# A hybrid encoder layer: the first 512 tokens turned and multiplied unscaled in the first pair of column tiles

## Chip, cores and metric

One Trainium2 chip, one core. The metric is the device time of one execution in microseconds (us), the median of several runs.

## What is computed

One encoder layer on x (1024 tokens x 1024 channels, float32), cut to what the change touches:

```
h    = x * rsqrt(mean(x*x over the channels) + 1e-6) * g_pre     # one inverse root for each token
proj = h @ w_in                                                  # 1024 x 7424 columns
q, k, v, gates, z, ... = split(proj)
q, k = partial_rope(q), partial_rope(k)                          # 16 of each head's 64 rows turn with the position
```

Behind it stand three branches (a short gated convolution; attention over a window of 128 tokens to each side, with a sink; cross-attention into 256 memory tokens), their up-projections, the merge by sigmoid gates, the output projection and `x + rms_norm(out)`. The inverse root of a token is a factor of its whole row of `h`, and so of its column in each tile of `proj`, which the kernel keeps transposed (channels on the partitions, tokens along the row).

## The kernel before

**Precision.** Each float32 operand is split into a high and a low float32r part. A product is three passes on TensorE: high x high, high x low, low x high. ScalarE makes the high parts (`high_part`, L1204, of weights; `high_of_h`, L1225, of h), and the low ones, operand minus high, are GpSimd's (`low_part`, L764; `low_of_h`, L769) or VectorE's.

**The start.** SyncE loads x in eight blocks of 128 tokens (L501 to L508), the weights of the first pair between them. ScalarE squares each block (`square_sum`, L1214; VectorE block 4), VectorE and ScalarE make the inverse roots (`variances`, `roots`, `inverses`), and the blocks are scaled in place: 0, 1, 2 and 4 by VectorE, 3, 6 and 7 by ScalarE, 5 by GpSimd. `turn_x` (L943) transposes chunk n: chunk 0 to 7 is 128 channels of tokens 0 to 511, 8 to 15 the same channels of tokens 512 to 1023. It takes four transposes into one of four PSUM banks (`spare`, by n % 4). From the bank ScalarE makes the high part with g_pre as its scale; VectorE makes the low part and, for n < 8, the float32 copy (`copy_h`, L1574); for n >= 8 the copy is ScalarE's (L1231). For the chunks of `POOL_CHUNKS` the low part is made by GpSimd from the copy. TensorE works off warm-up products (`warm`, L1082) in three batches until data are there.

**Column tiles.** The projection's 58 tiles of 128 columns go in pairs. The first three pairs (`P_DIRECT`) are multiplied directly: pair 0 by `first_pair` (L882), chunk by chunk, each chunk used for both tiles (six passes of 512 tokens), with the transposes of a later chunk ahead of it; pairs 1 and 2 by `direct_pair` (L907), a tile at a time, each of 48 + 48 passes over its two halves of weights. The rest are Strassen products (seven in place of eight), for which VectorE combines the four quarters of h: `sum_t1`, `sum_t3`, `sum_t2`, `sum_t4` (L1589 to L1612), each in four steps of 128x512.

**Order on VectorE.** Its list (L1725 to L1773) is worked off in this order: the lows and copies of the 16 chunks with the root work between them; T1 and T3, then T2, 12 sums; then for tile 0 (k) `swap_rows(0)`, `times_cos(0)`, `rotate(0)`: a shuffle of rows from PSUM, a product with the cosine table, one with the sine table and their sum, each 128x1024. The lows of combinations and the other four rotary tiles follow. A tile's PSUM bank is free when its cosine product is made: TensorE's tile 3 waits for `cos_made` 1, tile 4 for 2, tile 5 for 3 (L910 to L912). Only tiles T_K, T_Q to T_Q + 3 turn with the position; the first pair holds T_K and T_Q, and tile 2 is T_Q + 1.

**From the rotary tiles to attention.** ScalarE (`rope_high`, L1279) and GpSimd (`rope_low`, L785) split each tile, in their lists between parts of weights; SyncE stores the parts in DRAM (`store_rope`, L485) and, when the first four are stored, loads the first block for attention (`load_block(0)`, L541: q_d, kh_d, kl_d). TensorE's first scores (L977) wait for these three.

**Waits between engines** are on counted semaphores; each engine works its list strictly in order.

## Time and profile before

| | us |
|---|---|
| median of 3 runs (lowest, highest) | 926.87 (926.81, 927.2) |
| the profiled execution's own time | 925.96 |
| its span, first to last instruction | 924.1 |
| busy: TensorE / VectorE / ScalarE / GpSimd | 907.8 / 657.1 / 439.2 / 453.4 |
| mean granted TensorE clock | 0.996 |

The busy times are sums over the span. TensorE's is 98% of it, but the end of a matmul is modelled, so a busy engine need not be at its peak. A row of a timeline gives start, length, engine, line, operation, output and input; one that joins several instructions has their number behind an x. In a row the time in square brackets is idle time of the engine ahead of it.

### The profile page before, as it was taken

The page shows a single profiled execution, that of the slowest core. Times are in us where ns is not written, and L with a number is a line of the kernel's source. Part 1 is how long each engine was busy: PE and PEld are TensorE (multiplying, and loading weights), DVE is VectorE, ACT ScalarE, POOL GpSimd, SP SyncE. Part 2 cuts the span into 40 slices and gives each one's busy share as a digit, 9 for nine tenths or more (in the row PEclk, how much of TensorE's full clock was granted, in tenths as well). Part 3 has the DMA queues.
Part 4 walks back from the last instruction along what each step waited for, and adds up shares of the span by engine and source line. Part 5 has one row for each costly group of instructions (what it writes and reads, how often), then busy time and mean ns, then how long its engine had stood idle before and what let it go on. Part 6 is the DMA issues. An engine that isn't in the chain of part 4 may idle for free.

```text
span 924.1 us, 12763 instructions
## 1 busy us (share of the span) xinstructions
PE 907.8 (98%) x4376; PEld 763.3 (83%) x4376; DVE 657.1 (71%) x1060; ACT 439.2 (48%) x849; POOL 453.4 (49%) x303
## 2 busy tenths in 40 slices
PE   9999999999999999999999999999999999999995
PEld 8788788888888888888888888888888888888784
DVE  5689976565656566656576178888797358899887
ACT  7624464444444466544463434343444544445341
POOL 3546844444444444444446744444443636668452
PEclk9999999999999999999999999999999999999998
DMA  7243846252525242525255322222222974750333
GB/s 287 96 116 83 228 144 210 90 171 91 170 91 169 96 128 102 193 91 171 108 174 174 116 80 80 79 78 82 80 69 68 333 262 143 258 181 0 142 110 137
DMA packets 82336, 126.56 MB, mean 137 GB/s; under 512 B 7136, under 2 KB 40544, under 8 KB 82272
## 3 DMA queue, kind: packets, MB, share of 16 engines
q1 hardware_dynamic: 81952, 125.61, 41.2%
q8 instruction: 36, 0.59, 0.2%
q14 instruction: 28, 0.23, 0.1%
q10 hardware_dynamic: 320, 0.13, 0.1%
HBM read 92.56 MB, written 33.55 MB: 136 GB/s over the span
## 4 chain that ended last, share of the span: by engine, by line
PE 81%; DVE 8%; ACT 3%; DMA 3%; POOL 2%; issue 2%; SPq 1%; DVEq 0%; ACTq 0%
PE pm L866 17%; PE pm L864 17%; PE pm L865 17%; PE pm L1162 3%; PE pm L1163 3%; PE pm L1161 3%; PE pv L999 2%; PE sa L987 2%; PE sa L1163 2%; PE sa L1162 2%; PE sa L1161 2%; PE pv L1078 2%; PE sa L1058 1%; DVE area L2158 1%; DVE area L2135 1%
## 5 line engine op out<-in xcount | busy, mean ns | idle before, releaser
L766 POOL TENSOR_TENSOR ring<-spots,ring 128x512 fp32r<-128x512 f32 x234 | 340.9, 1460 | 389.9 <-ACT ring L1207 377.9
L864 PE MATMUL pm<-hc,ring 128*128 128x512 f32 x784 | 308.6, 394 | 0.0
L866 PE MATMUL pm<-hc,ring 128*128 128x512 f32 x784 | 305.8, 390 | 0.0
L865 PE MATMUL pm<-hc,ring 128*128 128x512 f32 x784 | 305.5, 390 | 0.0
L1207 ACT ACTIVATE ring<-spots 128x512 fp32r<-128x512 f32 x234 | 146.2, 628 | 268.6 <-PE pm L866 177.5
L866 PEld LDWEIGHTS pm<-hc,ring 128*128 128x128 f32 x784 | 147.2, 188 | 31.2
L864 PEld LDWEIGHTS pm<-hc,ring 128*128 128x128 f32 x784 | 147.3, 188 | 29.3 <-issue 0.6
L865 PEld LDWEIGHTS pm<-hc,ring 128*128 128x128 f32 x784 | 147.4, 188 | 28.9
L1161 PE MATMUL pm<-hc,ring 128*128 128x512 f32 x128 | 49.9, 390 | 0.0
L1162 PE MATMUL pm<-hc,ring 128*128 128x512 f32 x128 | 49.8, 389 | 0.0
L1163 PE MATMUL pm<-hc,ring 128*128 128x512 f32 x128 | 49.8, 389 | 0.0
L766 POOL TENSOR_TENSOR ring<-area,ring 128x512 fp32r<-128x512 f32 x28 | 41.6, 1484 | 12.2 <-ACT ring L1207 11.1
L1826 DVE TENSOR_TENSOR area<-pv,area 64x512 f32<-64x512 f32 x16 | 11.0, 689 | 49.1 <-ACT area L1334 49.1
L1664 DVE TENSOR_TENSOR snaps<-pm,snaps 128x512 f32<-128x512 f32 x26 | 17.9, 690 | 37.9 <-PE pm L866 37.8
L1457 ACT ACTIVATE area<-area 128x1024 f32<-128x1024 f32 x24 | 25.4, 1057 | 38.0 <-DMA area<-raw_d 38.0
L1212 ACT COPY snaps<-pm 128x512 f32<-128x512 f32 x26 | 15.3, 588 | 45.9 <-PE pm L866 45.9
L1341 ACT ACTIVATE area<-area,st 128x384 f32<-128x384 f32 (+1 forms) x64 | 36.7, 574 | 0.0
L1676 DVE TENSOR_TENSOR area<-pm,snaps 128x512 f32<-128x512 f32 x26 | 17.9, 690 | 24.4 <-PE pm L866 24.2
L1658 DVE TENSOR_TENSOR snaps<-pm,snaps 128x512 f32<-128x512 f32 x26 | 18.0, 691 | 23.3 <-PE pm L866 23.3
L1653 DVE TENSOR_TENSOR area<-pm,snaps 128x512 f32<-128x512 f32 x26 | 18.0, 692 | 21.7 <-PE pm L866 17.3
L1349 ACT ACTIVATE area<-area,st 128x384 f32<-128x384 f32 (+1 forms) x64 | 32.5, 579 | 0.8 <-DVE st L1812 0.6
L1628 DVE TENSOR_TENSOR spots<-spots 128x512 f32<-128x512 f32 x26 | 30.6, 1176 | 0.9
(248 smaller groups left out, 1664.5 us busy)
## 6 DMA issues: line engine op xcount, KB each, us to landing
spots<-in_w SPq DMA_DIRECT2D x116, 256.0 KB, 3.2
raw_d<-area SPq DMA_DIRECT2D x72, 256.0 KB, 2.0
area<-raw_d SPq DMA_DIRECT2D x24, 512.0 KB, 4.4
area<-in_x SPq DMA_DIRECT2D x16, 512.0 KB, 4.2
spots<-in_wup SPq DMA_DIRECT2D x24, 256.0 KB, 4.5
spots<-in_wout SPq DMA_DIRECT2D x20, 256.0 KB, 3.7
q_d<-area_r SPq DMA_DIRECT2D x16, 256.0 KB, 4.3
area<-raw_d SPq DMA_DIRECT2D x16, 256.0 KB, 3.6
```

The source lines that it names most:

```text
L766: nc.gpsimd.tensor_tensor(ring_part(n, 1), operand(n), ring_part(n, 0).bitcast(F32), ALU.subtract).then_inc(lo_made, 1)
L864: pe.matmul(bank, hi, moving_hi(k), start=(k == 0), stop=False)
L865: pe.matmul(bank, hi, moving_lo(k), start=False, stop=False)
L866: mm = pe.matmul(bank, lo, moving_hi(k), start=False, stop=(k == HC - 1))
L1161: pe.matmul(dst, hi, y[:, at, 0, cols], start=(begin and c == chunks[0]), stop=False)
L1162: pe.matmul(dst, hi, y[:, at, 1, cols], start=False, stop=False)
L1163: mm = pe.matmul(dst, lo, y[:, at, 0, cols], start=False, stop=(end and c == chunks[-1]))
L1207: nc.scalar.activation(ring_part(n, 0), operand(n), ACT.Copy).then_inc(hi_made, 1)
L1341: ins = nc.scalar.activation(row, row, ACT.Exp, bias=st[:, 3, h:h + 1], accum_out=st[:, 5, h:h + 1])
L1349: ins = nc.scalar.activation(row, row, ACT.Copy, scale=st[:, 6, h:h + 1])
L1457: nc.scalar.activation(gate_of(g), gate_of(g), ACT.Sigmoid).then_inc(gate_sig, 1)
L1628: nc.vector.tensor_tensor(spots[:, A21, :], spots[:, A11, :], spots[:, A21, :], ALU.subtract).then_inc(s_made, 1)
```

## The change

Tokens 0 to 511 are no longer scaled before they are turned. SyncE brings them in four pieces of 256 channels (`load_columns`), so that chunks 0 and 1 can be turned when the first piece is there; blocks 4 to 7 come by rows as before and are scaled before they are turned (4, 5 and 6 by VectorE, 7 by ScalarE). The first pair of tiles is multiplied with the unscaled chunks 0 to 7 in its first half. ScalarE now makes all 16 high parts and all 16 copies; of the squares, VectorE has blocks 4, 5, 7, 0 and 1 and ScalarE 6, 2 and 3. The inverse roots of tokens 0 to 511 are laid out as rows (`inverse_rows`) and spread over all partitions by four transposes into a PSUM bank (`spread_inverses`), ahead of chunk 13. With them VectorE scales the copies of chunks 0 to 7 (`normalise`), and their high and low parts are made once more (`high_of_normal`, `low_of_normal`, the latter on VectorE for chunks 0, 2, 4, 6 and on GpSimd for 1, 3, 5, 7); tile 2 runs its scaled second half of tokens first (`second_side`). The output of the first pair gets its factors in the rotary step: the first halves of the cosine and sine tables are multiplied by the inverse roots (`scale_tables`), and `times_cos` and `rotate` of the first two tiles go in two halves. The warm-up is one batch of 32 steps in place of 28, 8 and 4. Chunks from 8 on use three PSUM banks. Several semaphores are joined (memory and output variances and roots), with waits in the same places.

The diff, cut to its core:

```diff
-WARM_STEPS = (28, 8, 4)
-ROOT_GROUPS = (slice(0, 2), slice(2, 4), slice(4, NB))
-POOL_CHUNKS = (2, 6, 8, 10, 12, 14)
+WARM_STEPS = 32
+ROOT_GROUPS = (slice(4, 6), slice(6, NB), slice(0, 4))
+MEM_ROOT = len(ROOT_GROUPS) + 1
+POOL_CHUNKS = (4, 6, 10, 12, 14)
+POOL_NORMALS = (1, 3, 5, 7)
+TURNS_AT = {0: (), 1: (2, 3), 2: (4,), 3: (5,), 4: (6,), 5: (7,), 8: (9, 10), 9: (11,), 10: (12,), 11: (13,),
+            12: (14,), 13: (15,)}
+SPREAD_BEFORE = 13
+SQUARES = (4, 5, 7, 0, 1)
...
+def spare_of(n):
+    return n % 4 if n < KC else (n + 2) % 3
+def bank_before(n):
+    return n - 4 if n < KC else {KC: 5, KC + 1: 6, KC + 2: 4}.get(n, n - 3)
+def turn_no(n):
+    return n + 1 + (n >= SPREAD_BEFORE)
...
+        raw_cos, raw_sin = spots[:, S1, :], spots[:, S2, :]
...
+            def load_columns(pair):
+                cols = slice(2 * pair * P, 2 * (pair + 1) * P)
+                sp.dma_start(f32(X0, 4 * D).rearrange("p (b d) -> p b d", b=4)[:, :, cols],
+                             x[0:4 * P, cols].rearrange("(b p) d -> p b d", p=P)).then_inc(x_landed[pair], 16)
+            def load_x(b):
                 sp.dma_start(f32(X0 + b * D, D), x[b * P:(b + 1) * P, :]).then_inc(x_landed[b], 16)
+            load_spot(A11, 0)
+            load_columns(0)
             sp.dma_start(ident[:, :], ident_in).then_inc(ident_landed, 16)
             sp.dma_start(gpre[:, :], g_pre).then_inc(ident_landed, 16)
-            load_spot(A11, 0)
             load_spot(A21, 0)
-            for b in range(4, NB):
-                sp.dma_start(f32(X0 + b * D, D), x[b * P:(b + 1) * P, :]).then_inc(x_landed[b], 16)
+            load_columns(1)
             load_spot(A12, 0)
+            load_columns(2)
+            load_x(4)
             load_spot(A22, 0)
+            load_x(5)
+            load_columns(3)
+            load_x(6)
+            load_x(7)
...
+            sp.wait_ge(x_turned, 2 * KC + 1)
...
             nc.gpsimd.memset(snaps[:, 0, 0:P], 0.0).then_inc(warm_made, 1)
-            pool.wait_ge(xs_made, 2)
             low_part(0)
             low_part(1)
-            low_of_h(2)
             low_part(2)
             low_part(3)
-            pool.wait_ge(inv_made, 2)
-            nc.gpsimd.tensor_scalar(f32(X0 + 5 * D, D), f32(X0 + 5 * D, D), st[:, 9, 5:6], None,
-                                    ALU.mult).then_inc(xs_pool, 1)
-            for n in POOL_CHUNKS[1:]:
+            for n in POOL_CHUNKS:
                 low_of_h(n)
             low_part(4)
             low_part(5)
+            for n in POOL_NORMALS:
+                low_of_normal(n)
...
+                    for m in TURNS_AT.get(n, ()):
+                        if m == SPREAD_BEFORE:
+                            spread_inverses()
+                        turn_x(m)
...
+                        if n == KC - 1 and side == 1:
+                            turn_x(KC)
...
+            def second_side():
+                names = [(DIRECT[c], half) for half in (1, 0) for c in range(2)]
+                for name, half in names:
+                    n, c = AT[(1, name)], DIRECT.index(name)
+                    if half:
+                        pe.wait_ge(hi_made, n + 1)
+                        pe.wait_ge(lo_made, n + 1)
+                    elif c == 0:
+                        pe.wait_ge(n_hi, KC)
+                        pe.wait_ge(n_lo_pool, len(POOL_NORMALS))
+                        pe.wait_ge(n_lo_dve, KC - len(POOL_NORMALS))
+                    for k in range(HC):
+                        mm = direct(1, name, half, k, tile_bank(2), c == 0 and k == 0, c == 1 and k == HC - 1)
+                    if half == 0:
+                        mm.then_inc(slot_done, 1)
...
+            def spread_inverses():
+                pe.wait_ge(xs_made, 3)
+                pe.wait_ge(h_copied, KC)
+                pe.wait_ge(h_lo_dve, h_lo_count(KC - 1, h_lo_dve))
+                for b in range(4):
+                    mm = pe.transpose(pv[:, b * P:(b + 1) * P], snaps[:, 2, b * P:(b + 1) * P], ident[:, :])
+                mm.then_inc(x_turned, 1)
...
+            warm(WARM_STEPS)
             pe.wait_ge(ident_landed, 32)
-            for pair in range(2):
-                pe.wait_ge(xs_made, pair + 1)
-                if pair:
-                    pe.wait_ge(xs_act, 1)
-                for n in range(4):
-                    turn_x(n, (pair,))
-                warm(WARM_STEPS[pair + 1])
+            turn_x(0)
+            turn_x(1)
...
+                if n not in POOL_CHUNKS:
+                    act.wait_ge(h_lo_dve, h_lo_count(n, h_lo_dve))
+                nc.scalar.activation(f32(H_BLOCKS[n][2], HALF), spare[spare_of(n)], ACT.Identity,
+                                     scale=gpre[:, n % KC:n % KC + 1]).then_inc(h_copied, 1)
+            def high_of_normal(n):
+                idx, j, place = H_BLOCKS[n]
+                act.wait_ge(n_made, n + 1)
+                act.wait_ge(raw_used, 1)
+                nc.scalar.activation(hc[:, idx, 0, j, :], f32(place, HALF), ACT.Copy).then_inc(n_hi, 1)
...
-            for b in range(4):
-                square_sum(b)
-                if b % 2:
-                    roots(b // 2)
             high_part(0)
-            high_part(1)
-            act.wait_ge(inv_made, 1)
-            nc.scalar.activation(f32(X0 + 3 * D, D), f32(X0 + 3 * D, D), ACT.Copy,
-                                 scale=st[:, 9, 3:4]).then_inc(xs_act, 1)
             act.wait_ge(ident_landed, 32)
             for n in range(2 * KC):
                 high_of_h(n)
-                if n >= KC:
+                if n < 3:
+                    high_part(n + 1)
+                if n and n - 1 not in POOL_CHUNKS:
+                    copy_h(n - 1)
+                if n in POOL_CHUNKS:
                     copy_h(n)
-                if n == 1:
-                    square_sum(5)
-                if n == 2:
+                if n == 5:
+                    roots(0)
                     square_sum(6)
-                    high_part(2)
-                if n == 3:
-                    square_sum(7)
-                    high_part(3)
+                elif n == 6:
+                    roots(1)
+                elif n == 7:
+                    act.wait_ge(inv_made, 2)
+                    nc.scalar.activation(f32(X0 + 7 * D, D), f32(X0 + 7 * D, D), ACT.Copy,
+                                         scale=st[:, 9, 7:8]).then_inc(xs_act, 1)
+                elif n == 8:
+                    square_sum(2)
+                elif n == 9:
+                    square_sum(3)
+                elif n == 10:
                     roots(2)
-                if n == 5:
-                    act.wait_ge(inv_made, 2)
-                    for b in range(6, NB):
-                        ins = nc.scalar.activation(f32(X0 + b * D, D), f32(X0 + b * D, D), ACT.Copy,
-                                                   scale=st[:, 9, b:b + 1])
-                    ins.then_inc(xs_act, 1)
-                if n == 2 * KC - 2:
-                    high_part(4)
-                    high_part(5)
+                elif n in (13, 14):
+                    high_part(n - 9)
+            copy_h(2 * KC - 1)
+            for n in range(KC):
+                high_of_normal(n)
...
+            def low_of_h(n):
+                idx, j, _ = H_BLOCKS[n]
+                dve.wait_ge(h_hi_made, n + 1)
+                nc.vector.scalar_tensor_tensor(out=hc[:, idx, 1, j, :], in0=spare[spare_of(n)],
+                                               scalar=gpre[:, n % KC:n % KC + 1],
+                                               in1=hc[:, idx, 0, j, :].bitcast(F32), op0=ALU.mult,
+                                               op1=ALU.subtract).then_inc(h_lo_dve, 1)
+            def inverse_rows():
+                for b in range(4):
+                    ins = nc.vector.tensor_scalar(snaps[:, 2, b * P:(b + 1) * P], ident[:, :], 0.0, st[:, 9, b:b + 1],
+                                                  ALU.mult, ALU.add)
+                ins.then_inc(xs_made, 1)
+            def normalise(n):
+                place = f32(H_BLOCKS[n][2], HALF)
+                dve.wait_ge(x_turned, SPREAD_BEFORE + 1)
+                dve.wait_ge(h_copied, n + 1)
+                dve.wait_ge(h_lo_pool, h_lo_count(KC - 1, h_lo_pool))
+                nc.vector.tensor_tensor(place, place, pv[:, :], ALU.mult).then_inc(n_made, 1)
+            def low_of_normal(n):
                 idx, j, place = H_BLOCKS[n]
-                g = gpre[:, n % KC:n % KC + 1]
-                if n < KC:
-                    dve.wait_ge(h_hi_made, n + 1)
-                elif n % 2:
-                    dve.wait_ge(h_copied_act, n - KC + 1)
-                if n not in POOL_CHUNKS:
-                    nc.vector.scalar_tensor_tensor(out=hc[:, idx, 1, j, :], in0=spare[n % 4], scalar=g,
-                                                   in1=hc[:, idx, 0, j, :].bitcast(F32), op0=ALU.mult,
-                                                   op1=ALU.subtract).then_inc(h_lo_dve, 1)
-                if n < KC:
-                    nc.vector.tensor_scalar(f32(place, HALF), spare[n % 4], g, None, ALU.mult).then_inc(h_copied, 1)
+                dve.wait_ge(n_hi, n + 1)
+                nc.vector.tensor_tensor(hc[:, idx, 1, j, :], f32(place, HALF), hc[:, idx, 0, j, :].bitcast(F32),
+                                        ALU.subtract).then_inc(n_lo_dve, 1)
+            def scale_tables():
+                dve.wait_ge(rope_landed, 32)
+                for place, table in ((raw_cos, cosb), (raw_sin, sinb)):
+                    ins = nc.vector.tensor_tensor(place, table[:, 0:HALF], pv[:, :], ALU.mult)
+                link(ins)
...
                 b11, b12 = f32(B11F + j * HALF, HALF), f32(B12F + j * HALF, HALF)
-                dve.wait_ge(h_copied, j + 1)
-                dve.wait_ge(h_copied_act, j + 1)
-                dve.wait_ge(h_lo_pool, h_lo_count(HC, h_lo_pool))
+                dve.wait_ge(h_copied, KC + j + 1)
+                dve.wait_ge(n_made, j + 1)
+                dve.wait_ge(n_lo_pool, 2)
+                dve.wait_ge(n_lo_dve, 2)
...
+                if j < 2:
+                    nc.vector.tensor_tensor(rotated(j)[:, 0:HALF], tile_bank(t)[:, 0:HALF], raw_cos, ALU.mult)
+                    ins = nc.vector.tensor_tensor(rotated(j)[:, HALF:SEQ], tile_bank(t)[:, HALF:SEQ],
+                                                  cosb[:, HALF:SEQ], ALU.mult)
+                else:
+                    ins = nc.vector.tensor_tensor(rotated(j), tile_bank(t), cosb, ALU.mult)
...
+            low_of_h(0)
+            low_of_h(1)
+            low_of_h(2)
+            square_sum(4)
+            low_of_h(3)
+            square_sum(5)
             variances(0)
+            low_of_h(5)
             inverses(0)
-            scale_x((0, 1))
+            square_sum(7)
             variances(1)
+            scale_x((4, 5))
             inverses(1)
-            scale_x((2,))
-            square_sum(4)
-            for n in range(2 * KC):
-                copy_h(n)
-                if n == 3:
-                    variances(2)
-                    inverses(2)
-                if n == 4:
-                    scale_x((4,))
-                if n > KC + HC:
-                    sum_t1(n - KC - HC - 1)
-                    sum_t3(n - KC - HC - 1)
-            sum_t1(HC - 1)
-            sum_t3(HC - 1)
+            scale_x((6,))
+            low_of_h(7)
+            low_of_h(8)
+            square_sum(0)
+            low_of_h(9)
+            square_sum(1)
+            variances(2)
+            inverses(2)
+            inverse_rows()
+            low_of_h(11)
+            normalise(0)
+            normalise(1)
+            low_of_h(13)
+            for n in range(2, 5):
+                normalise(n)
+            low_of_h(15)
+            for n in range(5, KC):
+                normalise(n)
+            low_of_normal(0)
+            low_of_normal(2)
+            scale_tables()
+            low_of_normal(4)
+            low_of_normal(6)
+            for j in range(HC):
+                sum_t1(j)
+                sum_t3(j)
```

## Rows read from the trace of the kernel before

**Rows 1.** Waits of TensorE over the whole run: us in total, times, longest.

```profile
PE sa L864 <- DVE snaps L2186: 1.8, 1, 1.8
PE sa L977 <- DMA area_r<-kl_d: 1.5, 1, 1.5
...
PE pm L876 <- issue: 0.6, 1, 0.6
```

**Rows 2.** Stages: each engine's busy time, granted clock, DMA share, GB/s.

```profile
37.00:50.00 13.00, 13.00 (x61) 10.75 (x61) 13.00 (x14) 6.84 (x12) 8.44 (x5) 1.00 0.45 163
50.00:115.00 65.00, 63.47 (x285) 52.12 (x283) 60.37 (x69) 26.26 (x41) 43.56 (x23) 1.00 0.54 141
115.00:863.00 748.00, 747.84 (x3613) 630.79 (x3614) 513.22 (x871) 358.14 (x702) 360.60 (x245) 1.00 0.41 135
...
912.00:916.00 4.00, 2.10 (x10) 1.41 (x8) 3.48 (x5) 1.82 (x5) 0.00 (x0) 1.00 0.74 260
916.00:924.00 8.00, 0.00 (x0) 0.00 (x0) 4.39 (x11) 0.47 (x3) 0.00 (x0) 0.51 0.34 133
```

**Rows 3.** The chain of waits that ended last, up to 116 us: start, us, what.

```profile
2.11 6.94 DMA area<-in_x
...
31.19 0.44 PE pv L953 x4
...
48.20 1.82 DVE area L1607 x3
50.02 1.30 DVE area L1707
...
89.27 3.94 POOL hc L782 x2
...
108.61 6.14 DMA area_r<-kl_d
```

**Rows 4.** Stages of the warm-up, with the columns of rows 2.

```profile
0.00:4.80 4.80, 3.82 (x18) 3.83 (x19) 0.14 (x1) 2.17 (x3) 0.39 (x5) 1.00 0.62 227
4.80:9.40 4.60, 4.53 (x40) 4.33 (x39) 2.23 (x7) 3.30 (x8) 0.00 (x0) 1.00 0.89 311
```

**Rows 5.** Timeline: first products of pair 0, tile 2 and tile 3; first cosine product.

```profile
15.12 0.47 PE L876 MATMUL pm<-hc,ring 128*128 128x512 f32 x1 [0.28 <-DVE hc L1583]
...
44.24 0.39 PE L876 MATMUL sa<-hc,ring 128*128 128x512 f32 x1
...
51.22 1.21 DVE L1717 TENSOR_TENSOR area<-pm,area 128x1024 f32<-128x1024 f32 x1
...
55.12 0.39 PE L876 MATMUL pm<-hc,ring 128*128 128x512 f32 x1
```

**Rows 6.** Timeline: what one or two instructions of each kind take.

```profile
12.25 1.23 DVE L1549 CUSTOM_DVE_ANT_0 spots<-area 128x1024 f32<-128x1024 f32 x1
13.39 1.27 ACT L1228 ACTIVATE hc<-sa,gpre 128x512 fp32r<-128x512 f32 x2 [0.66 <-PE sa L953]
14.55 1.06 ACT L1217 ACTIVATE hc<-area 128x1024 fp32r<-128x1024 f32 x1
...
18.82 2.54 POOL L766 TENSOR_TENSOR ring<-spots,ring 128x512 fp32r<-128x512 f32 x2
...
23.14 0.74 DVE L1570 TENSOR_SCALAR area<-area,st 128x1024 f32<-128x1024 f32 x1
```

**Rows 7.** Timeline: VectorE beside GpSimd.

```profile
20.70 0.68 DVE L1538 SCALAR_TENSOR_TENSOR st<-st 128x4 f32<-128x4 f32 x1
...
40.29 3.44 POOL L766 TENSOR_TENSOR ring<-spots,ring 128x512 fp32r<-128x512 f32 x2
40.80 0.74 DVE L1583 SCALAR_TENSOR_TENSOR hc<-pv,gpre,hc 128x512 fp32r<-128x512 f32 x1
...
42.50 1.78 DVE L1599 TENSOR_TENSOR area<-area 128x512 f32<-128x512 f32 x1
44.20 0.68 DVE L1594 TENSOR_TENSOR area<-area 128x512 f32<-128x512 f32 x1
```

120 lines of the change are left out of this document (62 added, 58 removed).

## The prediction

> **What bounds the kernel now.** I read the waits of TensorE first, because the page has it busy for 98% of the span. Over the whole run it stands still for more than a microsecond only at a few places; the two that matter are 1.5 us at the first attention scores (L977), for a transfer of kl_d, and 1.8 us in the output phase [rows 1]. The table by stage says the same: from 115 us to 863 us TensorE is busy 747.84 of 748.00 us, from 50 to 115 us 63.47 of 65.00 [rows 2]. So the end is fixed by the time at which the scores start, 115.00 us, and whatever moves that time moves the end one for one: nothing behind it waits for anything that the change touches.
>
> Two things arrive there. TensorE itself arrives at about 113.5 us, 115.00 less its stall. The other is the chain of waits [rows 3]. Read it from the end: kl_d lands (108.61 + 6.14), behind it transfers of q_d, then low parts on GpSimd (two combinations from 89.27), the rotary low parts and their stores, back to the first row swap of the rotary part on VectorE at 50.02, and from there through VectorE's sums to about 37 us. Between 50 and 115 us there is no piece of TensorE in it. TensorE is 1.5 us ahead of this chain, so the scores wait for VectorE, GpSimd and the rotary transfers. From 37 to 50 us VectorE is busy 13.00 of 13.00 us [rows 2]: the start of the swap is its queue and nothing else. The change starts TensorE earlier; the question is when VectorE comes to `swap_rows(0)`.
>
> **The start of TensorE.** It works off 56 warm-up passes by 9.2 us: 18 by 4.8 us, one every 0.21 us, and from there one every 0.11 us, 40 instructions in 4.53 us [rows 4]. The new warm-up has 64 passes, 8 more, so it ends at 9.2 + 0.9 = 10.1 us. The first data don't bind: today four x blocks, 2 MB, have landed by 9.05 us [rows 3], and the new order needs 0.85 MB (weights, one column pair, the identity, g_pre). Column pairs come in pieces of 1 KB instead of 4; even at half the rate they would be there by about 8 us. Then 4 transposes, 0.65 us, a high part on ScalarE of 0.69, a low part on VectorE of 0.74, some 0.25 of semaphores: the first product at 12.5 us instead of 15.12 [rows 5, 6], 2.6 us earlier. Three groups of transposes (n = 2, n = 3 and the spread inverses) come into the stream: a group of four takes 0.44 us [rows 3], 1.3 in all. A step of six passes takes 1.37, six times the 0.228 at which the rows follow each other: the 48 passes of tile 2 from 44.24 to 55.12 us are 0.227 each [rows 5]. Without a stall the first pair would end at 12.5 + 16 x 1.37 + 15 x 0.44 = 41.0 us; it ends at 44.24 today [rows 5].
>
> **It will not run without a stall.** ScalarE now makes all 16 high parts and all 16 copies at 0.58 us a step, with four high parts of weights, three squares (1.06 each) and a scaling (1.1) inside the pair [rows 6]. I carried each queue forward with these steps, an instruction starting at the later of its engine and its inputs. n0 12.5; n1 14.9; n2 16.7; `low_of_h(3)` stands behind `square_sum(4)`, which meets GpSimd's `low_part(3)`: n3 19.3. copy(3), copy(4) and GpSimd's low (1.27) put n4 at 21.9, n5 at 23.8, n6 at 25.4. `low_of_h(7)` stands on VectorE behind square 7, variances (24.1), two scalings that GpSimd's low holds back (26.7), inverses (27.5) and a third scaling (28.2): n7 29.1. Then ScalarE's squares 2 and 3 stand ahead of copy(8), copy(9): n8 32.1, n9 34.5, n10 38.1. `inverses(2)` waits for ScalarE's root at 36.7 and for GpSimd until 38.0, the inverse rows end at 39.2, low(11) at 39.9, copy(12) at 41.3, low(12) at 42.6: n11 40.4, n12 42.7, n13 44.5, n14 45.9, n15 47.3. The pair ends at 48.7 us, 4.4 later than today, and ScalarE's last copy at 46.8.
>
> **VectorE and GpSimd after the pair.** The eight `high_of_normal` follow on ScalarE at 0.52 to 0.58 a step, from 46.8 to 51. VectorE takes its first low of them at 47.9. Before `swap_rows(0)` it has 4 lows, 2 scaled tables and 12 sums, 18 instructions at 0.60 (three in 1.82 us [rows 3]) = 10.8 us. GpSimd has 4 lows and low parts 6 and 7 in this stretch. Where a VectorE instruction with two SBUF operands meets one of GpSimd, each waits for the other to end: the sum at 42.50 takes 1.78 us beside GpSimd and the one at 44.20 0.68 alone, GpSimd's two take 3.44 in place of 2.54, and even an instruction of 4 columns, at 20.70, takes 0.68 [rows 6, 7]. Each GpSimd instruction so adds 1.78 - 0.60 = 1.15 us (rounded) to VectorE: 6 x 1.15 = 6.9. The Trainium skill, SBUF — State Buffer, section "Who interferes with whom", has this as an exclusive lock for a VectorE instruction with two SBUF inputs; by it the normalisations and tables, with one operand in PSUM, are free of it, and the trace agrees: the low part of h at 40.80, PSUM and SBUF, takes 0.74 beside GpSimd [rows 7].
>
> So the swap starts at 47.9 + 10.8 + 6.9 = 65.6 us instead of 50.02: 15.6 later. Bounds: nothing can start the lows before ScalarE has done its work. Counted without idle time from 10.8 us it has 27.6 us of it up to copy(15); with the 2 to 3 us that it waits at first, this gives 41.6 for the first low, 59.3 for the swap, +9.3. Without any meeting of the two engines but low parts 6 and 7 it is 41.6 + 10.8 + 2.3 = 54.7, +4.7. The other end: +17.5, if the stalls in the pair come out 2 us larger.
>
> **Small terms.** The ledger holds operations that no row shows. The inverse rows, 128x128: between nothing and the 0.74 of the 128x1024 scaling at 23.14 [rows 6] each; I take 0.2, nearer to the small end as they have an eighth of its columns, +0.8 in the ledger, 0 to 3.0. Rotary products split in halves: four more instructions while the chain is on VectorE, 0.05 each (an estimate: two starts in place of one), 0.2. The tables' load is issued after the spread (44.7 us) and lands by 49; it hides behind the normal lows and would cost its excess if those ran early. GpSimd's removed x scaling (2.9 us) and VectorE's eight removed copies are inside the ledger. Semaphores renamed: nothing; the waits are in the same places.
>
> **Sum.** Tile 3 on TensorE waits for the first cosine product, which ends 2.4 us after the swap begins: 68.0 against TensorE ready at 61, where the second side itself has waited 1.4 us for the normal lows. Today tile 3 starts at 55.12 and the product ends at 52.43 [rows 5], so 2.7 us of cover are gone and TensorE is 13 us later; it comes to the scores at 126.4. The chain comes at 115.0 + 15.6 = 130.6 and decides, and TensorE's new wait there is 4.2 us. The chain's 15.6 and the 0.2 of the halves: made against the profiled execution, 925.96 us (span 924.1 and 1.9 around it), this is 941.8; that execution lies 0.9 us under the median, so the median of the runs should come to 926.87 + 15.8 = **942.7 us**. A measurement of this kernel tells about 0.2%, 1.9 us, from no change.
>
> **Rivals.**
> (a) The pair runs nearly free: swap at 55 to 61, +5 to +11, 932 to 938 us. For it: the orders of ScalarE and VectorE could mesh better than my ledger, whose stalls hang on a few tenths. Chance 0.17.
> (b) The clock falls. After TensorE's last product (busy 2.10 us from 912) the granted clock is 0.51 from 916 on, the lower of its levels, 1.2 GHz; the stalls of 1.5 and 1.8 us left it at 1.00 [rows 1, 2]. A wait of 4.2 us at the scores could give the low level back, and the warm-up shows the price: 18 passes at 0.21 instead of 0.11, 1.9 us on the end, 944.6. The Trainium skill, TensorE: Matmul & The Clock Gate, section "What's actually happening", has activity releasing the clock and idle time taking it back; by it the long waits would lose it. At tile 3 it would cost nothing, as TensorE isn't the chain there. Chance 0.22.
> (c) The other side: the early start carries through. TensorE would reach the scores at 113.5 - 2.6 + 1.3 - 0.6 (its longest present stall in the pair [rows 1]) = 111.6 and save up to 3.4 us: 923.5. But the chain would have to come earlier too: for a gain over 1.9 us the swap must start by 48.1, so the sums by 40.9. The queue has the normal lows ahead of the sums, and these wait for all of the pair's turns, 37 us at the earliest, and 4.2 us of ScalarE. Chance 0.04, for a misreading of the queue.
> (d) The change doesn't reach the chain, the delays cancel: 0.02.
> The forecast has 0.55. The range, 934 to 946, takes in (b), most of (a) and the larger stalls.
>
> **What would show it.** The first product near 12.5; first pair's end near 48.7, `swap_rows(0)` near 65.6 with sums of 1.78 us between 50 and 65; a wait of TensorE at tile 3 for VectorE's cosine product of 5 to 7 us; the scores near 130.6 after a wait of 3 to 5; behind them the same 748 us. If the swap is before 52 us, my reading is wrong; if it is at 65 and the scores aren't 15 later, the chain has slack that I didn't see.

## The result and the profile after

Four runs of each, in turn on one chip: 941.22 us median (940.19 to 943.57) after, 926.84 us (926.38 to 927.2) before; ratio 1.0159, 95% interval [1.0138, 1.018]. The kernel is 14.4 us slower (12.8 to 16.7 by the interval); the forecast was 942.7 us, 15.8 slower.

The profiled execution took 943.57 us (span 941.7). Its waits of TensorE, in the columns of [rows 1]:

```profile
PE pm L912 <- DVE area L1815: 6.0, 1, 6.0
...
PE pv L900 <- POOL ring L802: 1.4, 1, 1.4
PE sa L1044 <- DMA area_r<-area_r: 1.4, 1, 1.4
```

L1815 is the second half of the first cosine product; L912 behind it is tile 3, which did not wait before. The wait at the scores (L1044) is what it was, 1.4 us against 1.5. The next rows are the timeline of TensorE: first product, chunks 7 and 10, tile 2, its scaled half, tile 3 with the pass behind it, and the pass with which the 0.23 us step is back.

```profile
13.24 0.47 PE L912 MATMUL pm<-hc,ring 128*128 128x512 f32 x1 [1.47 <-ACT hc L1291]
...
29.13 0.47 PE L912 MATMUL pm<-hc,ring 128*128 128x512 f32 x1 [1.08 <-DVE hc L1649]
...
38.26 0.47 PE L912 MATMUL pm<-hc,ring 128*128 128x512 f32 x1 [1.38 <-ACT hc L1291]
...
48.98 0.39 PE L912 MATMUL sa<-hc,ring 128*128 128x512 f32 x1
...
55.48 0.47 PE L912 MATMUL sa<-hc,ring 128*128 128x512 f32 x1 [0.90 <-DVE hc L1672]
...
67.19 0.80 PE L912 MATMUL pm<-hc,ring 128*128 128x512 f32 x1 [5.98 <-DVE area L1815]
67.78 0.63 PE L913 MATMUL pm<-hc,ring 128*128 128x512 f32 x1
...
71.17 0.39 PE L912 MATMUL pm<-hc,ring 128*128 128x512 f32 x1
```

The pair starts 1.9 us earlier than before [rows 5] and ends 4.7 later, at 48.98. VectorE's timeline from there to the swap is the core of the case: two normal lows, the two tables, two more lows, the first three sums, the last four, the swap of rows and the second half of the cosine product.

```profile
48.25 2.42 DVE L1672 TENSOR_TENSOR hc<-area,hc 128x512 fp32r<-128x512 f32 x2
50.59 1.27 DVE L1679 TENSOR_TENSOR spots<-area,pv 128x512 f32<-128x512 f32 x2
51.90 3.44 DVE L1672 TENSOR_TENSOR hc<-area,hc 128x512 fp32r<-128x512 f32 x2
55.26 1.77 DVE L1688 TENSOR_TENSOR area<-area 128x512 f32<-128x512 f32 x1
56.95 1.78 DVE L1693 TENSOR_TENSOR area<-area 128x512 f32<-128x512 f32 x1
58.66 0.68 DVE L1688 TENSOR_TENSOR area<-area 128x512 f32<-128x512 f32 x1
...
62.27 2.48 DVE L1701 TENSOR_TENSOR area<-area 128x512 f32<-128x512 f32 x4
...
64.69 1.28 DVE L1803 STREAM_SHUFFLE area<-pm 128x1024 f32<-128x1024 f32 x1
...
66.46 0.67 DVE L1815 TENSOR_TENSOR area<-pm,area 128x512 f32<-128x512 f32 x1
```

VectorE has no idle time in it. Beside it GpSimd runs its four normal lows (6.40 us from 48.38) and low parts 6 and 7:

```profile
48.38 6.40 POOL L815 TENSOR_TENSOR hc<-area,hc 128x512 fp32r<-128x512 f32 x4
54.75 3.43 POOL L802 TENSOR_TENSOR ring<-spots,ring 128x512 fp32r<-128x512 f32 x2
```

The chain of waits that ended last, with the columns of [rows 3], has no TensorE between the swap and the scores. It goes at first as before, through VectorE, the first rotary low part on GpSimd and its stores. Its last part is another than in [rows 3]: VectorE up to the last rotary tile, that tile's high part on ScalarE, and the last of four short transfers that ScalarE issues itself.

```profile
62.87 1.82 DVE area L1701 x3
64.69 1.27 DVE area L1803
...
70.76 2.92 POOL area_r L826
...
77.97 4.69 DMA kl_d<-area_r
...
118.03 1.07 ACT area_r L1354
...
123.34 6.08 DMA area_r<-area_r
...
129.62 0.36 PE sa L1044
```

The two branches end almost together: the load of kl_d, with which the chain ended before, takes 6.10 us here and lands at 129.37, the transfer shown at 129.42 (before: 114.75 and 114.55). From the swap to the scores it is 64.93 us (129.62 - 64.69), before 64.98 (115.00 - 50.02 [rows 2, 3]). The scores come 14.62 us later, and the medians lie 14.4 apart; the dates are those of one execution of each kernel. The profiled execution is the longest of its four and has 3.0 us more behind the scores. The 3.0 us are a wait of 1.4 us for GpSimd's low part at 854.38, and 1.6 us of TensorE's low clock behind the old wait of the output phase, a pass every 0.43 us where it is 0.23 otherwise. The last row has the columns of [rows 2]: the granted clock from 894 to 897 us is 0.50.

```profile
854.38 0.47 PE L900 MATMUL pv<-hc,ring 128*128 128x512 f32 x1 [1.40 <-POOL ring L802]
...
892.29 0.50 PE L900 MATMUL sa<-hc,ring 128*128 128x512 f32 x1 [1.82 <-DVE snaps L2313]
...
894.29 0.63 PE L901 MATMUL sa<-hc,ring 128*128 128x512 f32 x1
...
894.00:897.00 3.00, 3.00 (x9) 2.32 (x8) 2.72 (x5) 1.24 (x3) 0.81 (x2) 0.50 0.46 172
```

### The profile page after: what moved, and what is told of

It is laid out like the page before. It is cut to its first block, busy times and chain, and to the rows that moved or that the text cites. A ratio compares the mean times of both kernels' runs of the same rounds, so it can differ in the third digit from the quotient of the medians.

```text
span 941.7 us, 12804 instructions
## 1 busy us (share of the span) xinstructions
PE 912.7 (97%) x4364; PEld 764.3 (81%) x4364; DVE 670.6 (71%) x1082; ACT 441.4 (47%) x855; POOL 453.6 (48%) x305
## 4 chain that ended last, share of the span: by engine, by line
PE 66%; DVE 12%; DMA 7%; issue 5%; ACT 2%; POOL 1%; SPq 1%; ACTq 0%; DVEq 0%
PE pm L902 17%; PE pm L900 17%; PE pm L901 17%; DMA area<-raw_d 4%; PE pv L1066 2%; PE sa L1054 2%; PE pv L1145 1%; PE sa L1125 1%; DVE area L2183 1%; DVE area L2181 1%; PE sa L1044 1%; PE sa L1046 1%; ACT area L1527 1%; DMA area<-in_g_post 1%; PE sa L1133 1%
## 5 line engine op out<-in xcount | busy, mean ns | idle before, releaser
L900 PE MATMUL pm<-hc,ring 128*128 128x512 f32 x784 | 308.7, 394 | 0.6 <-POOL ring L802 0.6
L902 PE MATMUL pm<-hc,ring 128*128 128x512 f32 x784 | 305.8, 390 | 0.0
L901 PE MATMUL pm<-hc,ring 128*128 128x512 f32 x784 | 305.5, 390 | 0.0
L1223 PE MATMUL pm<-hc,ring 128*128 128x512 f32 x128 | 49.9, 390 | 0.0
L1224 PE MATMUL pm<-hc,ring 128*128 128x512 f32 x128 | 49.8, 389 | 0.0
L1225 PE MATMUL pm<-hc,ring 128*128 128x512 f32 x128 | 49.8, 389 | 0.0
L802 POOL TENSOR_TENSOR ring<-area,ring 128x512 fp32r<-128x512 f32 x28 | 42.6, 1528 | 14.4 <-ACT ring L1269 13.7
L912 PE MATMUL pm<-hc,ring 128*128 128x512 f32 x64 | 27.1, 423 | 11.9 <-DVE area L1815 6.0
```

The source lines that it names most:

```text
L802: nc.gpsimd.tensor_tensor(ring_part(n, 1), operand(n), ring_part(n, 0).bitcast(F32), ALU.subtract).then_inc(lo_made, 1)
L900: pe.matmul(bank, hi, moving_hi(k), start=(k == 0), stop=False)
L901: pe.matmul(bank, hi, moving_lo(k), start=False, stop=False)
L902: mm = pe.matmul(bank, lo, moving_hi(k), start=False, stop=(k == HC - 1))
L912: pe.matmul(dst, hi, hc[:, idx, 0, k, :], start=first, stop=False)
L1223: pe.matmul(dst, hi, y[:, at, 0, cols], start=(begin and c == chunks[0]), stop=False)
```

## The experiments

Theory A: the time follows the first row swap one to one, and the swap starts when VectorE has worked off the items ahead of it. Twelve kernels test this and its parts. Each was measured beside runs of the kernel before; its median in that session is in the last column. Columns three to six are us of the profiled execution.

| run | median, us | first product | first swap | tile 3 | scores | ratio to before [95%] | before |
|---|---|---|---|---|---|---|---|
| before | 926.84 | 15.12 | 50.02 | 55.12 | 115.00 | | |
| after | 941.22 | 13.24 | 64.69 | 67.19 | 129.62 | 1.0159 [1.0138, 1.018] | 926.84 |
| e1_before_delay | 934.75 | 14.90 | 58.53 | 60.97 | 122.78 | 1.0095 [1.0076, 1.0114] | 926.15 |
| e2_hoist | 939.73 | 13.68 | 55.71 | 61.48 | 128.18 | 1.0149 [1.0134, 1.0165] | 926.15 |
| e3_dve_normals | 940.09 | 13.02 | 63.63 | 66.14 | 128.70 | 1.0157 [1.0136, 1.0179] | 926.15 |
| e4_no_normals | 935.24 | 12.29 | 58.00 | 60.52 | 122.62 | 1.0107 [1.0091, 1.0122] | 926.15 |
| e5_kl_first | 926.38 | 14.72 | 49.64 | 54.77 | 114.60 | 1.0006 [0.9997, 1.0014] | 926.15 |
| e6_warm20 | 937.19 | 9.59 | 60.39 | 62.89 | 124.35 | 1.0123 [1.0108, 1.0139] | 926.15 |
| e7_no_squares | 940.38 | 12.99 | 62.38 | 64.88 | 128.56 | 1.0153 [1.0139, 1.0167] | 926.15 |
| e8_mended | 938.39 | 10.54 | 53.89 | 61.20 | 127.44 | 1.0135 [1.0121, 1.0148] | 926.15 |
| e9_parts_late | 939.21 | 12.51 | 61.76 | 64.29 | 127.09 | 1.0138 [1.0123, 1.0153] | 926.95 |
| e10_three | 934.43 | 9.44 | 57.32 | 59.85 | 122.02 | 1.009 [1.0073, 1.0107] | 926.95 |
| e11_before_parts_late | 924.91 | 15.08 | 47.80 | 55.09 | 113.11 | 0.9981 [0.9972, 0.999] | 926.47 |
| e12_before_both | 923.99 | 14.81 | 47.39 | 54.72 | 112.75 | 0.9977 [0.9968, 0.9987] | 926.47 |

The medians of the kernel before differ by up to 0.8 us between the sessions, so a time is compared by its loss, the median less that of the kernel before beside it: 14.4 us for the kernel after, and in e2 to e4 13.6, 13.9 and 9.1, in e6 to e10 11.0, 14.2, 12.2, 12.3 and 7.5. By the intervals of their ratios only e4 and e10 are apart from the kernel after, and e6 just touches it. What e2, e3, e7, e8 and e9 gain is read from the dates of one profile each.

These dates carry a scatter of their own, at the start: TensorE's warm-up passes change from one every 0.21 us to one every 0.11 at 3.9 us in one profile and at 7.1 in another. The six profiles with the start of the kernel after (after, e2, e3, e4, e7, e9) change between 4.3 and 7.1 us and have their first product, in the same order, between 12.29 and 13.68. So a first swap that comes earlier has to be split into the part that the first product already has and the rest.

**e1_before_delay**: the kernel before with idle work ahead of the swap.

```diff
+            for _ in range(12):
+                link(nc.vector.tensor_tensor(spots[:, S2, :], spots[:, S1, :], spots[:, S1, :], ALU.mult))
             swap_rows(0)
```

> The kernel before with 12 idle products of 128x512 (about 0.65 us each with their links, 7.8 in all) put on VectorE just ahead of the first row swap; nothing else changed. Theory A (the chain from the swap over the rotary parts to the scores has no slack): swap at 57.8 instead of 50.0, scores at 122.8 instead of 115.0, time 934.6 us, and TensorE stands 2 to 5 us at tile 3. Rival B (the loss of the change comes from TensorE's own stalls in the first pair, and a late swap is covered): 927 to 929 us.

```profile
49.81 8.67 DVE L1749 TENSOR_TENSOR spots<-spots 128x512 f32<-128x512 f32 x12
...
58.53 1.29 DVE L1707 STREAM_SHUFFLE area<-pm 128x1024 f32<-128x1024 f32 x1
```

In the kernel before the swap comes 8.5 us later, the scores 7.8, the time 8.6 (934.75 - 926.15). So VectorE's queue alone, with nothing of the change, sets the time at close to one to one. TensorE's wait at tile 3 is 5.9 us, where 2 to 5 were expected.

**e2_hoist**: the first rotary tile ahead of the 12 sums, in the kernel after.

```diff
             low_of_normal(6)
+            swap_rows(0)
+            times_cos(0)
+            rotate(0)
             for j in range(HC):
                 sum_t1(j)
...
                 sum_t2(j)
-            swap_rows(0)
-            times_cos(0)
-            rotate(0)
```

> The changed kernel with the first tile's row swap, cosine product and rotation moved ahead of the 12 sums. Theory A: TensorE's 6.0 us stall at tile 3 goes, because its cosine product is made by 57 to 58 us; but the high part of the first rotary tile needs the sums T2 and starts at 69 to 70 us as before, so the scores stay within 1.5 us of 129.6 and the time within 2 us of 941.2. Rival C (the 6 us at tile 3 are what is lost): 935 us.

The first swap is 9.0 us earlier and TensorE's wait of 6 us at tile 3 is gone. Yet the scores come only 1.4 us earlier: the sums stand behind the first rotary tile now, and the second swap comes 14.5 us after the first (in the kernel before 9.35, 50.02 to 59.37), at 70.21. In the kernel after it is at 74.16, and of these 3.95 us, too, only 1.1 are left at the fifth swap, 99.47 against 100.55.

```profile
65.39 2.49 DVE L1701 TENSOR_TENSOR area<-area 128x512 f32<-128x512 f32 x4
67.80 2.49 DVE L1713 TENSOR_TENSOR hc<-area,hc 128x512 fp32r<-128x512 f32 x4
...
70.21 1.34 DVE L1803 STREAM_SHUFFLE area<-pm 128x1024 f32<-128x1024 f32 x1
```

The visible wait of TensorE was a sign of the delay and not its cause. What sets the time is the whole of VectorE's list, of which the first swap is a good marker only while the order stays. The fifth swap, the last, is the better one: in the twelve profiles in which the scores wait for a transfer they come 28.4 to 29.2 us after it, e2 and e8 among them, and 30.0 in e7; after the first swap it is 64.0 to 73.6.

**e3_dve_normals**: all eight second low parts on VectorE.

```diff
-POOL_NORMALS = (1, 3, 5, 7)
+POOL_NORMALS = ()
```

(and the counts of the waits and VectorE's list to match)

> The changed kernel with all eight second low parts on VectorE, GpSimd's four among them. Theory A (a VectorE instruction with two SBUF operands and one of GpSimd exclude each other, so GpSimd's four cost VectorE 1.15 us each): VectorE has 4 x 0.60 more and 4 x 1.15 less less one meeting that was partly hidden, the swap comes 0.5 to 2 us earlier than 64.7, time 939 to 941. Rival D (GpSimd's work beside VectorE is free, only VectorE's count matters): swap 2.4 us later, time 943.6.

```profile
48.05 2.53 DVE L1671 TENSOR_TENSOR hc<-area,hc 128x512 fp32r<-128x512 f32 x4
50.50 1.27 DVE L1678 TENSOR_TENSOR spots<-area,pv 128x512 f32<-128x512 f32 x2
51.81 4.67 DVE L1671 TENSOR_TENSOR hc<-area,hc 128x512 fp32r<-128x512 f32 x4
56.40 0.68 DVE L1686 TENSOR_TENSOR area<-area 128x512 f32<-128x512 f32 x1
```

VectorE makes four instructions more and comes to the swap 1.05 us earlier, 0.85 of it between tile 2 and the swap (14.86 us instead of 15.71). Four lows alone take 2.53; the four that meet low parts 6 and 7 take 4.67, and the sums none of the 1.78. The time, 940.09, can't be told from that of the kernel after.

**e4_no_normals**: without the second split of chunks 0 to 7.

```diff
-            for n in range(KC):
-                high_of_normal(n)
...
-            low_of_normal(0)
-            low_of_normal(2)
             scale_tables()
-            low_of_normal(4)
-            low_of_normal(6)
```

(without the `normalise` calls and GpSimd's normal lows too)

> The changed kernel without the second split: the eight scalings of the copies, their eight high and eight low parts are left out, so the first 512 tokens stay unscaled in everything but the first pair's outputs. Theory A: the sums start when the tables are there, at about 51 us, the swap at 58.3 instead of 64.7, scores at 123.2, time 935 us: the second split costs 6.4 us and the later first pair the rest, about 8 us. Rival B (the first pair's stalls on TensorE set the time): within 1 us of 941.2.

```profile
49.09 1.29 DVE L1674 TENSOR_TENSOR spots<-area,pv 128x512 f32<-128x512 f32 x2 [3.48 <-DMA area<-in_sin]
...
58.00 1.29 DVE L1794 STREAM_SHUFFLE area<-pm 128x1024 f32<-128x1024 f32 x1
```

As expected: swap 58.00, 6.7 earlier, scores 122.62. But 0.95 of the 6.7 is the early first product of this profile (12.29); between tile 2 and the swap it is 9.93 us instead of 15.71, 5.8 less, and the loss is 5.3 less. So the second split costs 5.3 to 5.8 us, some 40% of the loss. The tables' load, which the prediction costed at nothing behind the normal lows and at its excess without them, is what VectorE waits for here, 3.5 us.

**e5_kl_first**: a try to shorten the chain in the kernel before. VectorE's third and fourth cosine products wait there for the stores of an earlier rotary tile; the stores of k's low part go first, and the third waits for them alone.

```diff
+                for g in range(2 if c is None else 0):
+                    own = slice(g * HEAD, (g + 1) * HEAD)
+                    sp.dma_start(kl_d[own, g, :], low[own, :]).then_inc(zero_stored, 16)
                 for g in range(2):
...
-                        sp.dma_start(kl_d[own, g, :], low[own, :]).then_inc(done, 16)
```

> The kernel before with the two stores of the first tile's low part (kl_d) issued ahead of its four kh_d stores, counted by themselves, so that the third cosine product waits for these two alone. Theory A (the scores wait for this chain): VectorE's 2.3 us of idle time ahead of that product go, the chain comes about 2 us earlier, TensorE's stall at the scores (1.5 us) goes, scores at 113.5, time 1.3 to 1.7 us under the kernel before. Theory of a chain with slack elsewhere: no change.

No gain. The wait of 2.3 us for the stores is gone, but the fourth swap starts at 77.77, in the kernel before at 76.33. The first three rows are of e5, the last two of the kernel before:

```profile
66.29 4.54 DVE L1618 TENSOR_TENSOR area<-area 128x512 f32<-128x512 f32 x4
70.75 7.09 DVE L1623 TENSOR_TENSOR hc<-area,hc 128x512 fp32r<-128x512 f32 x8
77.77 0.01 DVE L1713 LOAD_MASK_SELECT area<-pm  x1
...
71.51 4.90 DVE L1617 TENSOR_TENSOR hc<-area,hc 128x512 fp32r<-128x512 f32 x8
72.85 4.71 POOL L766 TENSOR_TENSOR ring<-spots,ring 128x512 fp32r<-128x512 f32 x1 [3.82 <-ACT ring L1207]
```

In the kernel before the same four sums take 2.49 us from 69.10 and the same eight lows 4.90. Moved earlier, they meet four instructions of GpSimd and lose 4.2 us to them. A wait of 1.5 us for weights, behind the fourth swap, goes in return, and the fifth swap is at 85.63, in the kernel before at 85.80: gain and loss cancel. To run beside GpSimd is not always to be held: the eight lows of the kernel before do so too, and there it is GpSimd's low part that takes 4.71 us. No run here shows what decides which of the two is held.

**e6_warm20**: 20 warm-up steps of two passes in place of 32.

```diff
-WARM_STEPS = 32
+WARM_STEPS = 20
```

> The changed kernel with 20 warm-up steps instead of 32, 24 passes fewer, 2.7 us. Theory A (the pair and VectorE's queue behind it are a fixed length from the first product on): first product 2.0 to 2.7 us earlier, tile 2 and the swap earlier by the same, time 938.5 to 939.5. Rival E (the x blocks or the weights bind the pair): first product earlier, tile 2 within 0.5 us of where it was, time 941.

```profile
9.59 0.47 PE L912 MATMUL pm<-hc,ring 128*128 128x512 f32 x1 [1.48 <-ACT hc L1291]
```

First product 3.65 us earlier, swap 4.3, scores 5.3; the loss is 3.3 us smaller. I had expected 2.0 to 2.7 for the start. 24 passes at 0.11 are 2.65 of the 3.65; the other 1.0 is the clock, which was low for longer in the profiled run of the kernel after (15 passes between 4.8 and 7.0 us, here 22). The pair takes 35.12 us instead of 35.74. So the time follows the swap, but to no better than about 1 us.

**e7_no_squares**: without the squares of tokens 0 to 511.

```diff
-                elif n == 8:
-                    square_sum(2)
-                elif n == 9:
-                    square_sum(3)
...
-            square_sum(0)
             low_of_h(9)
-            square_sum(1)
```

> The changed kernel without the squares of blocks 0 to 3, two on ScalarE (1.04 us each) and two on VectorE (1.22); the inverse roots of tokens 0 to 511 are then those of a zero sum. Theory A (the pair is slow because root work stands on ScalarE and VectorE between the chunks): the pair, 35.75 us from the first product to tile 2, gets 2 to 3 us shorter, the swap and the time come 2 to 3 us earlier, 938 to 939. Rival F (TensorE's own work and the transposes set the pair): 35.75 stays, 941.2.

The pair takes 33.73 us (from the first product to tile 2) instead of 35.74, the 2.0 expected, and the swap is 2.3 earlier. The time isn't 2 to 3 us lower: the loss is 0.2 smaller, and in the profile the scores come only 1.1 earlier. The last transfer ahead of them, the load of kl_d, took 6.88 us in this profile, 6.14 in that of before [rows 3] and 5.80 in e10_three:

```profile
121.43 6.88 DMA area_r<-kl_d
```

Against the same load in the kernel after (6.10) that is 0.8 of the missing 1.2 us. TensorE's wait at the scores is so 2.3 us long, and passes at the low clock follow it up to 132.0 us. That the other runs of this kernel lose the same is not shown.

**e8_mended**: the kernel after with e2, e3, the 20 steps and the stores of e5 together.

> The changed kernel with all that so far brought something: second low parts on VectorE, first tile's rotary work ahead of the sums, 20 warm-up steps, kl_d stores first. Theory A, if the gains add: 1.1 + 1.4 + 2.5 + 2.2 = 7 us, 934 us; the second split and the longer pair stay, so it does not reach 926.9.

Missed by 4.4 us, and no better than e6 alone. First and second swap are at 53.89 and 68.37, 14.5 apart as in e2, and from the second to the scores it is 59.1 us, in e10 55.1 (122.02 - 66.93). The hoist and the earlier stores give back what the rest gains. The two were not taken out one by one; from the third swap to the fourth it is 14.9 us here, 12.7 in e2 with the hoist alone and 11.9 in e10 with neither, and e5, with the stores alone, has 13.8 where the kernel before has 12.0.

**e9_parts_late**: the two low parts that met the sums are held back.

```diff
                 low_of_normal(n)
+            pool.wait_ge(sum_made[T2], HC)
             low_part(6)
```

> The kernel after the change, with GpSimd's sixth and seventh low part of the first input tile held until VectorE's twelve products of x with the inverse roots are done, so that they no longer meet. Theory A (two-source products of VectorE and GpSimd hold each other up; each low part that meets the products costs VectorE about 1.15 us): the first swap falls about 2.3 us earlier, near 62.4 instead of 64.7; tile 3 starts near 65, its low parts being ready by then; the scores start near 127.3 and the time is near 939. Rival R (the products take what they take because of their own operands, and GpSimd only waits): the first swap stays at 64.7, and the two held low parts come later on GpSimd, so tile 3 starts at 67 or later and the time stays at 941.2 or above.

```profile
54.52 0.68 DVE L1689 TENSOR_TENSOR area<-area 128x512 f32<-128x512 f32 x1
55.13 0.68 DVE L1694 TENSOR_TENSOR area<-area 128x512 f32<-128x512 f32 x1
```

The expectation calls the twelve sums products of x with the inverse roots; the hold is on the last of the sums. The same two sums as at 55.26 and 56.95 take 0.68 instead of 1.77 and 1.78. From tile 2 to the swap it is 13.52 us instead of 15.71: two meetings, 2.2 us, by one line that adds no work. The loss is 2.1 us smaller. (The swap, 2.9 earlier, has another 0.7 from the first product.)

**e10_three**: e3, e6 and e9 together, without hoist and stores.

> The kernel after the change with three edits at once: 20 warm-up steps, all eight second low parts on VectorE, and GpSimd's sixth and seventh low part held until the twelve products are done. Theory A (the delay of the first swap is the sum of the items ahead of it, and the time follows it one to one): 937.2 with the short warm-up alone, less 1.1 for the normals on VectorE, less 2.3 for the two meetings, 933.8 in all, first swap near 57, scores near 121. That is still 7 us above the kernel before. Rival G (what is gained ahead of the first swap is given back behind it, in later waits of VectorE or in a later landing of the transposed rows, as far as other combinations did): 936 to 937, with the swap near 57 but the scores at 123 or later.

```profile
47.67 2.50 DVE L1672 TENSOR_TENSOR hc<-area,hc 128x512 fp32r<-128x512 f32 x4
...
57.32 1.30 DVE L1801 STREAM_SHUFFLE area<-pm 128x1024 f32<-128x1024 f32 x1
```

934.43 against 933.8 expected, the scores at 122.02 where 121 was expected: these three add up. Between tile 2 and the swap it is 12.67 us, 3.0 less than in the kernel after, which is the 0.85 of e3 and the 2.19 of e9. No instruction of VectorE is held any longer in this stretch. The swap is 7.3 us behind that of the kernel before. 0.4 of it is a later tile 2, at 44.65; the rest is the longer list behind it.

**e11_before_parts_late** and **e12_before_both**: the line of e9 in the kernel before, alone and with the stores of e5.

```diff
             low_part(5)
+            pool.wait_ge(sum_made[T2], HC)
             low_part(6)
```

> The kernel before the change, with GpSimd's sixth and seventh low part held until VectorE's twelve sums are done; today they start at 44.53 us and meet two of the sums. Theory A: the first swap comes 1.2 to 2.3 us earlier, near 48.3 instead of 50.02, and the chain to the scores with it, but TensorE itself arrives at 113.5, so that the scores can gain no more than their present stall of 1.5 us: scores near 113.6, time 925.4 against 926.9. Rival G (gained time is given back behind the swap, as when the DMA waits of VectorE were taken away): scores between 114.6 and 115.2, time within 0.5 us of the kernel before. Rival T: the two parts now reach tile 3 too late or meet the sine product and the sum of the first rotary tile, and the time is 1 to 3 us above the kernel before.

> The kernel before the change with the same hold of the two low parts, and with the low stores of k first, so that VectorE's third cosine product waits for these alone. Theory A (the chain gets shorter by the sum of both): the scores are then bound by TensorE's arrival at 113.5, no stall is left at L977, time 925.3 against 926.9, not below the hold alone by more than 0.3. Rival G: no gain, scores between 114.6 and 115.2, time within 0.5 us of the kernel before.

```profile
44.78 0.68 DVE L1600 TENSOR_TENSOR area<-area 128x512 f32<-128x512 f32 x1
45.38 2.48 DVE L1608 TENSOR_TENSOR area<-area 128x512 f32<-128x512 f32 x4
...
47.80 1.33 DVE L1708 STREAM_SHUFFLE area<-pm 128x1024 f32<-128x1024 f32 x1
```

Both are faster than both kernels: e11 by 1.56 us (interval of the ratio below 1), e12 by 2.48; their intervals overlap. e12 is 0.9 us below e11 where at most 0.3 was expected; as its first product happened to come 0.3 earlier, it stays open whether the stores add anything. In e11 the swap is 2.2 earlier, but the time gains 1.6: in e11 no wait is left at the scores, and TensorE goes from tile 3 to them in 58.02 us, before in 59.88 with 1.5 of waiting. As expected, TensorE itself is the bound there now.

## Why the prediction was right, and where it was off

**The bound.** Right: TensorE's waits and its busy share pointed at the scores, and the chain at VectorE's queue. e1, e6 and e10 bear it out to about 1 us: 8.6, 3.3 and 6.9 us of time for 8.5, 4.3 and 7.4 of the swap. e2 shows its limit: it holds for delays of the whole list.

**The start.** Forecast 12.5, measured 13.24 with the clock late, 12.51 in e9 with the same start: the step is right. Its scatter, 12.29 to 13.68 in six profiles, was not in it.

**The ledger of the pair.** Chunks 7, 10 and tile 2 were forecast at 29.1, 38.1 and 48.7 and came at 29.13, 38.26 and 48.98, though the start was 0.7 late, so the pair itself is 0.5 shorter than forecast, and that the dates agree so closely is in part luck. Its length, 35.74, is the same within 0.05 us in e2, e3, e4, e8 and e9, and 35.1 to 35.2 in e6 and e10. That ScalarE's and VectorE's work sets part of it is shown by e7, whose pair is 2.0 shorter; that their orders set all of it is not shown. The unstalled 28.5 of rival (a) is nowhere near.

**VectorE behind the pair.** Start 47.9 forecast, 48.25 measured; 18 instructions, 10.8, right. The meetings were mis-sized: forecast six at 1.15 us, 6.9; measured 16.44 - 10.8 = 5.6, five meetings, because one of GpSimd's normal lows ran beside the two table products, which took 1.27 us together and were not held. The forecast had named these as free and then counted the meeting all the same. So the swap was at 64.69 and not at 65.6. The Trainium skill, SBUF — State Buffer, section "Who interferes with whom", has the lock for VectorE instructions with two SBUF inputs and, apart from perf modes that use both ports, not for those with one. The trace agrees: the table products read PSUM and took 0.6 us each beside GpSimd, the normal lows with two SBUF operands up to 1.78. The scalings of blocks 4 and 5, which have one large SBUF input and a column of factors, were held as well, 2.44 us for two where one takes 0.74 alone [rows 6]; the prediction's ledger had this. No run shows whether they ran in such a mode.

```profile
24.44 2.44 DVE L1641 TENSOR_SCALAR area<-area,st 128x1024 f32<-128x1024 f32 x2
```

**Behind the swap.** Tile 3's wait for the cosine product: 5 to 7 forecast, 6.0 measured. The halves were put at +0.2; the whole stretch to the scores is 0.05 shorter, so they cost nothing that shows. That the stretch keeps its length so exactly is luck: the chain ends through another transfer than before, and from the first swap to the scores the other kernels with the same order have 64.0 to 66.2 us. TensorE was to wait 4.2 us at the scores and waited 1.4: the chain came 1.0 earlier than forecast, and TensorE 1.8 later. Its passes from 67.78 to 71.17 took 3.4 us where eight take 1.8 at the usual step, and it had a wait of 0.6 for GpSimd at 117.06. Over those passes the granted clock is 0.50, the lower of its two levels, 1.2 GHz (columns of [rows 2]):

```profile
67.80:71.10 3.30, 3.30 (x9) 2.62 (x8) 3.27 (x5) 1.47 (x2) 0.34 (x1) 0.50 0.00 0
```

Only 1.4 us of cover were left.

**Rivals.** (b), the fall of the clock, happened, but at tile 3, where the forecast had it free of cost; it was, barely. At the scores its condition, a wait of 4.2 us, was not met. (c) would have needed the swap by 48.1: e4 shows that even without the second split it would be at 58. (d), no effect, is out: the swap is at 64.69 and the scores are 14.6 later.

**The 14.7 us by which the swap is later.** Tile 2 comes 4.7 us later: the first product is 1.9 earlier and the pair 6.6 longer. From tile 2 to the swap it is 15.71 us instead of 5.78, 9.9 more. Of the 9.9 the second split is 5.8 (e4) and the meetings with low parts 6 and 7 are 2.2 (e9), but the kernel before has such meetings too, worth 2.2 in e11. One difference in order is seen in the rows: seven of the twelve sums had started by tile 2 in the kernel before, and none here. What that alone costs was not measured. In the pair the four squares are 2.0 (e7); the rest of the 6.6 was not taken apart. Twelve warm-up steps less would start everything some 2.7 us earlier (e6).

## What to carry to other kernels

An earlier start of the busiest engine is worth nothing when a side engine's list sets a later date: date the last item of that list before and after, and count what the change adds to it. Look in the timeline for instructions of VectorE that take 1.1 us more than their twins, and ask whether the GpSimd instruction beside them is due now; one wait that moved two such instructions out of the way brought the swap 2.2 us forward in both kernels (and 1.6 us of time in the kernel before), where moving four instructions from GpSimd to VectorE brought 0.8 (e3). When a wait on the chain is taken away, look at what the work that moves forward will meet: in e5 and e8 it met GpSimd, and the gain was gone.

## What the runs showed of the hardware

**The clock and the length of a wait.** Waits are as the rows give them. From the first product on, waits of up to 1.58 us were never followed by a slower step than 0.23 us. The wait in the output phase (1.77 to 1.82 us) was followed by 7 or 8 passes at 0.43 us in 5 of the 14 profiles (after, e5, e9, e11, e12) and by none in the other 9. All waits of 2.19 us and more (the longest in after, e1, e6 and e7, 5.9 to 6.0 us) were followed by such passes, 6 to 13 of them. The Trainium skill, TensorE: Matmul & The Clock Gate, section "What's actually happening", has the clock as gated by activity with two levels; the step is at either 0.23 or 0.43 us here, nothing steady between. The same wait can go either way, and eight such passes cost 1.6 us. How much of the scatter between runs of one kernel is due to it is not shown, as each kernel has one profile.

**The same transfer, other times.** The load of kl_d ahead of the scores took between 5.43 (e1) and 6.88 us (e7) in the 14 profiles; which transfers ran beside it was not compared. The wait at 854.38 in the kernel after is not in every profile: e1, e4 and e3 have it with 1.2, 1.2 and 0.6 us, and the other ten profiles do not.
